# Second mixer: one modulation's weighted sum moved from VectorE to ScalarE and adding transfers

## The reference, cut to what matters

```
c_act = silu(c)                       # 1024 numbers
mod   = c_act @ w_ada + b_ada         # 6 x 1024: shift, scale, gate twice
```

## Time and profile before

| What | us |
|---|---|
| Median of 3 runs | 1464.32 |
| Lowest and highest run | 1462.7, 1465.55 |
| Span of the profiled execution, first to last instruction | 1458.9 |
| PE busy in it | 1373.3 (94%) |
| DVE busy in it | 873.2 (60%) |
| ACT busy in it | 252.0 (17%) |
| POOL busy in it | 258.8 (18%) |

### The profile page before, as it was taken

How to read it: one execution, slowest core, us unless ns; L and a number is a source line. 1 busy time by engine, 2 the same in 40 slices (tenths; PEclk the granted TensorE clock), 3 DMA queues, 4 the chain that set the end, 5 groups by cost and what they waited for, 6 DMA issues and landing times. The chain is left out here.

```text
span 1458.9 us, 18939 instructions
## 1 busy us (share of the span) xinstructions
PE 1373.3 (94%) x7533; PEld 1013.0 (69%) x7533; DVE 873.2 (60%) x1502; ACT 252.0 (17%) x540; POOL 258.8 (18%) x342
## 2 busy tenths in 40 slices
PE   5999999887766999999999999999999999999997
PEld 1877655554433788868888888777776878888843
DVE  2458685442222668763454685788763874777864
ACT  2221121000001211222345101000002113211101
POOL 5078010000000200453355402100020100000000
PEclk9999999998998999999999999999999999999999
DMA  9976878999999598856774455898864552555531
GB/s 350 319 258 229 283 307 347 363 416 415 417 418 378 181 316 277 298 162 164 161 179 132 158 163 175 326 336 311 303 230 141 155 157 80 163 164 171 172 129 46
DMA packets 176055, 355.57 MB, mean 244 GB/s; under 512 B 7289, under 2 KB 137040, under 8 KB 158560
## 3 DMA queue, kind: packets, MB, share of 16 engines
q1 hardware_dynamic: 166720, 313.64, 60.6%
q0 software_dynamic: 9248, 40.71, 9.5%
HBM read 352.58 MB, written 1.74 MB: 243 GB/s over the span
## 5 line engine op out<-in xcount | busy, mean ns | idle before, releaser
L1824 PE MATMUL PS<-HT,ring 128*128 128x256 f32 x1152 | 258.3, 382 | 0.1
L1824 PEld LDWEIGHTS PS<-HT,ring 128*128 128x128 f32 x1152 | 215.4, 190 | 36.0 <-issue 7.9
L1542 DVE TENSOR_TENSOR X<-X,PS 128x1024 f32<-128x1024 f32 x14 | 17.1, 1221 | 112.0 <-PE PS L1318 112.0
L1265 PE MATMUL PS<-ring_extra,slot_rows 128*32 128x256 f32 x576 | 55.2, 440 | 27.7 <-DMA ring_extra<-in_expert_w_gate 7.0
L2758 PE MATMUL PS<-HT,ring 128*128 128x256 f32 x352 | 76.8, 379 | 0.0
L2787 PE MATMUL PS<-ada_stage,half_sums 128*128 128x256 f32 x320 | 75.6, 379 | 0.0
L2787 PE MATMUL PS<-ring,half_sums 128*128 128x256 f32 x320 | 75.6, 379 | 0.0
L2758 PEld LDWEIGHTS PS<-HT,ring 128*128 128x128 f32 x352 | 66.7, 190 | 9.0
L2764 PE MATMUL PS<-ring,hid 128*128 128x512 f32 x160 | 71.8, 592 | 0.0
L2787 PE MATMUL PS<-ring,HT 128*128 128x256 f32 x304 | 68.8, 379 | 0.0
L2787 PEld LDWEIGHTS PS<-ring,half_sums 128*128 128x128 f32 x320 | 59.4, 190 | 11.2 <-issue 4.3
(11 more groups left out here) (713 smaller groups left out, 2450.5 us busy)
## 6 DMA issues: line engine op xcount, KB each, us to landing
ring<-in_hy_w_in SPq DMA_DIRECT2D x40, 1024.0 KB, 7.5
ring_extra<-in_w_ada SPq DMA_DIRECT2D x24, 1024.0 KB, 8.0
ada_stage<-in_ada_w POOLq DMA_DIRECT2D x24, 1024.0 KB, 7.4
ring<-in_ffn_w_gate SPq DMA_DIRECT2D x22, 1024.0 KB, 5.8
ring<-in_ffn_w_up SPq DMA_DIRECT2D x22, 1024.0 KB, 5.7
ring<-in_ffn_w_down SPq DMA_DIRECT2D x22, 1024.0 KB, 6.0
ring_extra<-in_expert_w_down SPq DMA_DIRECT2D x18, 1024.0 KB, 22.9
ring_extra<-in_expert_w_up SPq DMA_DIRECT2D x18, 1024.0 KB, 20.1
```

Of the source, the lines that this page charges most:

```text
L1265: mm = pe.matmul(PS[e * SLOTS:(e + 1) * SLOTS, 2, j * CW:(j + 1) * CW], hs[:, k, e * SLOTS:(e + 1) * SLOTS], w[e][:, k, :], start=(k == 0) ...
L1542: dve.tensor_tensor(part, part, PS[:, 6:8, :], ALU.add).then_inc(added, 1)
L1824: mm = pe.matmul(dst, w[:, k, half * P:(half + 1) * P], HT[:, k, :], start=(k == 0), stop=(k == KT - 1))
```

## The change

The staging place is doubled: `stages` has two, and piece `a` goes to place `a % 2`. Fetch `a` stands one step earlier in SP's list than before. ACT multiplies a piece with its column, in place, at (a + 2, 3), where DVE's `add(a)` was; for k = 0 it writes into `acc` instead. For the 14 pieces with k from 1 to 7, POOL then starts, at the head of the next step, a transfer from the staging place to `acc` that adds at its destination. Fetch `a` waits, for a = 2 and 3, until piece a - 2 has been multiplied into `acc`; from a = 4 on, until the adding transfer of piece a - 2 has landed. PE waits at (19, 2) for the last two adding transfers. DVE's `add` is gone.

```diff
-        stage = sb(scope, "ada_stage", [P, 2 * D])
+        stages = sb(scope, "ada_stage", [P, 2, 2 * D])
+        stage = stages[:, 0]
-        add_at = {(s, 3): s - 2 for s in range(2, 18)}
+        weigh_at = {(s, 3): s - 2 for s in range(2, 18)}
 # SP
-                    for (step_no, _), a in add_at.items():
-                        if step_no == s + (s > 0) or (s == 0 and step_no <= 1):
-                            if a:
-                                sp.wait_ge(summed, a)
-                            sp.dma_start(stage[:].rearrange("p (a n) -> p a n", a=1), wv[:, ds(a // 2, 1), 1 + a % 2, :])\
-                                .then_inc(fetched, 16)
+                    for (step_no, _), a in weigh_at.items():
+                        if step_no == s + (2 if s else 0) or (s == 1 and step_no == 2):
+                            if 2 <= a < 4:
+                                sp.wait_ge(weighed, a - 1)
+                            elif a >= 4:
+                                sp.wait_ge(summed[a % 2], 16 * (a // 2 - 1))
+                            sp.dma_start(stages[:, a % 2:a % 2 + 1, :], wv[:, ds(a // 2, 1), 1 + a % 2, :])\
+                                .then_inc(fetched[a % 2], 16)
 # PE, at (19, 2)
-                        pe.wait_ge(summed, ADDS)
+                        for j in range(2):
+                            pe.wait_ge(summed[j], 16 * (KT - 1))
 # ACT, called at each (s, q) in weigh_at, before that quarter's exponential
+                def weigh(a):
+                    j, k = a % 2, a // 2
+                    act.wait_ge(fetched[j], 16 * (k + 1))
+                    if a == 0:
+                        act.wait_ge(cv_ok, 1)
+                    act.activation(acc[:, j, :] if k == 0 else stages[:, j, :], stages[:, j, :], ACT.Copy,
+                                   scale=cv[:, k:k + 1]).then_inc(weighed, 1)
 # DVE
-                def add(a):
-                    j, k = a % 2, a // 2
-                    dve.wait_ge(fetched, 16 * (a + 1))
...
-                        dve.scalar_tensor_tensor(out=acc[:, j, :], in0=stage[:], scalar=cv[:, k:k + 1], in1=acc[:, j, :],
-                                                 op0=ALU.mult, op1=ALU.add).then_inc(summed, 1)
 # POOL, called at (s, 0) of the step after weigh(a), for a >= 2, ahead of that step's other jobs
+                def add(a):
+                    j, k = a % 2, a // 2
+                    pool.wait_ge(weighed, a + 1)
+                    if k >= 2:
+                        pool.wait_ge(summed[j], 16 * (k - 1))
+                    pool.dma_start(acc[:, j, :], stages[:, j, :], accum_op=ALU.add).then_inc(summed[j], 16)
```

More of the change, by code:

```diff
@@ L1646, in _program @@
         wdt = sb(scope, "w_dt", [P, KT, SSM_H])
-        dt_parts = sb(scope, "dt_parts", [P, S])
+        dt_parts = cum_bias[:, 2016:2016 + S]
         quarter_sum = sb(scope, "quarter_sum", [P, SSM_H])
@@ L1673, in _program @@
         bias_dram = nc.dram_tensor("bias_rows_dram", (ATT_G * KV_H, 384), F32, kind="Internal").ap()
-        small, stored = pool_dma_sem("a_small"), pool_dma_sem("a_stored")
+        small, stored, SMALLS_BEFORE = smalls1, pool_dma_sem("a_stored"), 48
         def small_loads(pool):
@@ L1696, in small_loads @@
                     pool.dma_start(dst, src).then_inc(small, 16)
-        SMALLS = 16 * 16
+        SMALLS = SMALLS_BEFORE + 16 * 16
         xg = carve(x_scores, 0, [TT, D])
@@ L1704, in _program @@
             sem("g_left"), sem("g_right"))
-        late, padded = pool_dma_sem("a_late"), sem("h_padded")
+        padded = sem("h_padded")
         x_squared, x_out = sem("g_xsquared"), sem("o_xout")
@@ L1738, in _program @@
             sem("s_weight"), sem("s_value"), sem("s_ymoved"))
-        cum_out, cum_in = pool_dma_sem("cum_out"), [pool_dma_sem(f"cum_in{j}") for j in range(3)]
-        bias_in = [pool_dma_sem("bias_in0"), pool_dma_sem("bias_in1")]
+        cum_in, CUMS_BEFORE = (smalls2, smalls3, gates_in), (160, 96, 32)
+        bias_in, BIAS_BEFORE = (r_small, pool_dma_sem("bias_in1")), (96, 0)
         scored, biased, maxed, probs, added, scaled, turned, copied, valued, moved_att = (
@@ L1774, in y_block @@
             return YT[:, g * KT + 4 * h:g * KT + 4 * h + 4, i * P:(i + 1) * P]
-        cv_ok, fetched, summed, cols, cols_ok, rows_a, rows_b, gate_ok = (
-            sem("d_c"), sem("d_fetched"), sem("d_summed"), sem("d_cols"),
-            sem("d_colsok"), sem("d_rows_a"), sem("d_rows_b"), sem("d_gates"))
+        cv_ok, fetched, weighed, summed, cols, rows_a, rows_b, gate_ok = (
+            sem("d_c"), [sem("d_fetched0"), sem("d_fetched1")], sem("d_weighed"),
+            [pool_dma_sem("d_summed0"), pool_dma_sem("d_summed1")], sem("d_cols"),
+            sem("d_rows_a"), sem("d_rows_b"), sem("d_gates"))
         row_sums, row_copies = sem("d_rowsum"), sem("d_rowcopy")
@@ L2110, in _ @@
                         act.activation(cv[:], cv[:], ACT.Silu).then_inc(cv_ok, 1)
+                    if (s, q) in weigh_at:
+                        weigh(weigh_at[s, q])
                     if q == 2 and 2 <= s < 2 + NX:
@@ L2246, in setup @@
                     dve.wait_ge(made, 1)
-                    dve.tensor_copy(dt_parts[:], PS[:, 5, 0:S]).then_inc(dt_moved, 1)
+                    dve.tensor_copy(dt_parts, PS[:, 5, 0:S]).then_inc(dt_moved, 1)
                     dve.tensor_copy(convT[:], PS[:, 7, 0:(CONV + 1) * XT])
@@ L2357, in _ @@
                         softplus()
-                    if (s, q) in add_at:
-                        add(add_at[s, q])
                     if (s, q) == (6, 0):
@@ L2374, in _ @@
                         if h < SSM_H:
-                            dve.wait_ge(cum_in[h // 4 % 3], 16 * (h // 12 + 1))
+                            dve.wait_ge(cum_in[h // 4 % 3], CUMS_BEFORE[h // 4 % 3] + 16 * (h // 12 + 1))
                             if h >= 3:
@@ L2387, in _ @@
                         dve.wait_ge(rows_a, 1)
-                        dve.wait_ge(late, 16)
+                        dve.wait_ge(small, SMALLS + 16)
                         dve.tensor_tensor(gate_a[:], gate_a[:], PS[:, 2:4, :].rearrange("p a b -> p (a b)"), ALU.add)\
@@ L2411, in _ @@
                             dve.wait_ge(scored, k + 1)
-                            dve.wait_ge(bias_in[m % 2], 32 * (m // 2 + 1))
+                            dve.wait_ge(bias_in[m % 2], BIAS_BEFORE[m % 2] + 32 * (m // 2 + 1))
                             if k >= 2:
@@ L2478, in load_cums @@
                     if p == 0:
-                        pool.wait_ge(cum_out, 16)
-                        pool.wait_ge(stored, 16)
+                        pool.wait_ge(stored, 32)
                         pool.wait_ge(la_ok, 1)
@@ L2489, in _ @@
                 pool.wait_ge(n_gained, TT)
-                pool.dma_start(gate_a[:], t["ada_b"][0][2 * D:3 * D].partition_broadcast(P)).then_inc(late, 16)
+                pool.wait_ge(small, SMALLS)
+                pool.dma_start(gate_a[:], t["ada_b"][0][2 * D:3 * D].partition_broadcast(P)).then_inc(small, 16)
                 for s, q in QUARTERS:
+                    if (s - 1, 3) in weigh_at and q == 0 and weigh_at[s - 1, 3] >= 2:
+                        add(weigh_at[s - 1, 3])
                     if (s, q) == (2, 0):
@@ L2496, in _ @@
                         pool.wait_ge(cum_mv, 2)
-                        pool.dma_start(cum_dram, cumT[:]).then_inc(cum_out, 16)
+                        pool.dma_start(cum_dram, cumT[:]).then_inc(stored, 16)
                         for p in range(3):
```

## The result

The changed kernel takes 1497.48 us where the kernel before, run beside it, takes 1464.93: a ratio of 1.0232 (95% interval 1.0211 to 1.0254), so it is slower by 2.1 to 2.5%, some 34 us. The ratio is an estimate of its own and not the quotient of the two medians, which is 1.0222, or 32.6 us. The forecast was 1473.9, slower by 9.6. The side was right and the place was right; the forecast was about three and a half times too small.

A forecast was written before the change was run, and what follows sets the result against it. PE was taken to bound the steps the change touches; a 1458.9 us span, 9.6 us of PE waiting on a too-long staging loop and 5.4 up to the runs' median gave 1473.9 us, range 1461.5 to 1511.

The forecast's parts named there:

- PE bounds, DVE's work is worth nothing: Steps from 480 to 640 us: PE sets their time, so taking 36.6 us busy off DVE gains 0.
- ACT's multiplication at 1.9 us: ACT's 16 multiplications of 128x2048: 1.9 us each, bounds 1.3 to 2.4, 30 us on an idle engine, 0 by itself.
- Where PE waits and from what x on: PE waits behind ACT's multiplication of piece 14, latest start 615.8 us; nothing up to x = 15.1, 9.6 us at 16.7.
- x: One turn of the staging loop over two steps, without ACT's 1.9 us multiplication: 16.7 us, from 10.8 to 22.9.
- E: PE's wait from late pieces after six loop turns: 6x - 90.6 us, 9.6 us at x = 16.7.
- The terms of x: Staging loop, issue and landing times in one turn: 0.3 + 9.9 + 0.3 + 6.2 = 16.7 us.
- ACT's end to POOL's issue: Staging loop, from the multiplication's end to the start of the adding transfer: 0.3 us.
- adding transfer, issue to SP's next fetch: Staging loop: 1 MB addition 9.9 us to land, upper bound 14.8; 0.3 for landing to SP's issue and to ACT together.
- fetch, issue to ACT's start: Staging loop, 1 MB fetch beside ring tile and adding transfer: 6.2 us, the middle of 4.9 and 7.5.
- The cross-check by throughput: DMA over 12 steps of 7.9 us: at 418 GB/s 7.5 us a step fits; 10.0 with destination reads costs +18 us.
- what ACT may be late: ACT's multiplication of piece 14 may slip from 608.4 to 615.8 us: 7.4 us taken off the 26 us lack.
- The rival "saturation": DMA transfers in these steps: addition and fetch at upper bounds, x = 22.9, E = 46.8, time 1511 us; chance 0.18.

The follow-up runs named there:

- the third experiment: The changed kernel with ACT multiplying in the two places but DVE adding the product, no adding transfers: 1462.2 us, ratio 0.9989.
- the four places: The changed kernel with four staging places in place of two, a fetch waiting for the adding transfer of piece a - 4: 1493.45 us, ratio 1.0197.
- the kernel with copies: The changed kernel with plain copies in place of the adding transfers, same bytes and waits, no sum: 1473.76 us, ratio 1.0063.

## Why the prediction was off, step by step

**PE bounds, DVE's work is worth nothing: right.** DVE lost 31.2 us of busy time over the whole span (873.2 to 842.0), and nothing became faster; with DVE adding again, the time is that of before.

**ACT's multiplication at 1.9 us: right** (2.00), and harmless, as the third experiment shows.

**Where PE waits and from what x on: right.** The working took the even pieces. The odd ones decide: ACT waited for the landing of each odd piece from 5 to 15. For them the same sum starts at the end of piece 3's multiplication: 521.27 + 1.99 + 5 x 2.0 + 6x. It gives the measured start of piece 15, 658.88, for x = 20.9. Piece 15 stands one step later than piece 14; in the kernel before, PE's heads of that step start at 629.17, and the same count back from there gives about 625 as the latest start. So E is 34 us: that is the loss. By this sum PE waits from x = 15.3 on, where I had 15.1, and my own 16.7 gives 8.5 us. The wait chain, its place, and ACT as the engine behind which it piles up were as forecast.

**The terms of x: the step that failed.** I had 16.7 where 20.9 was measured. The timelines give the starts of the six odd turns: POOL's issues at 523.56, 549.07, 573.62, 594.12, 614.89 and 638.41 us, SP's next fetches at 535.45, 561.95, 584.23, 604.46, 625.06 and 648.89, ACT's multiplications at 546.77, 571.21, 591.83, 612.52, 634.98 and 658.88. The means are:

| Term | Forecast, us | Measured, us |
|---|---|---|
| ACT's end to POOL's issue | 0.3 | 0.5 |
| adding transfer, issue to SP's next fetch | 9.9, and 0.3 for this hop and the next | 11.1 (10.2 to 12.9) |
| fetch, issue to ACT's start | 6.2 | 9.4 (7.6 to 11.3) |

The fetch is the term that failed: 3.2 of the 4.2 us that x was short lie there. I had taken a middle between two landings of a time when no third transfer was there. The addition was 1.2 us longer than 9.9, and between its landing and SP's issue nothing was lost. At six turns, each us of x is 6 us. Behind the sizes stands an idea that failed with them: I took each landing as a length that a transfer has by itself, and the runs showed that in this stage it goes with the sum of engine time that all transfers of a step want.

**The cross-check by throughput: it should have caught this, and failed by its price.** I divided bytes by 418 GB/s, the best rate of any slice, in a stage with other traffic, and got 7.5 to 10.0 us a step. This stage's own rows had the price: two loads took 0.82 of a 7.34 us step, which is 6.0 us of the engines, not the 5.0 that 418 GB/s gives. With a double-priced addition on top a step wants 11. By that I would have written about 30 us and not 18. In both I took 7.4 us off for what ACT may be late; the table above takes nothing off. The decay rows' eight loads, 0.52 MB each, want about 11 us of the same engines and were in no sum of mine; that they use up the allowance is worked out, not shown.

**The rival "saturation" was the mechanism.** It had 0.18 and a price of 46.8, from upper bounds. Its sign was to be ring tiles on which PE waits; they landed late (13.2 us), but with six slots PE never waited for one, and the loss came through ACT. So most of the signs that I had listed for the forecast (ACT's waits for `ada_stage`, PE's gaps ended by ACT and POOL, additions of 10.5 us in the median, a DMA share above 0.95) were there, for another reason than latency: the four places show that. Two were not: the fetch landed after 8.9 us and not about 6, and ACT's waits did not grow from piece to piece (7.41, 14.77, 12.00, 12.02, 9.42 and 9.63 us for the odd ones). That the side and the place came out right under the wrong mechanism was in part luck: both mechanisms delay the landings that ACT waits for.

The Trainium skill's sentence in "DMA: Bandwidth & Descriptors", section "Issuing engines are not separate DMA queues", that transfers of all engines end on the same 16 and interleave, is what these runs show: shares of 55.0 and 48.3% in one window, and a ring tile at 13.2 us. The other sentence that I took from this page of the Trainium skill, section "Anatomy of one DMA", gives by its fit an estimate of 4.4 us for 1 MB. No 1 MB copy or addition here landed so early: the shortest copy took 5.0 us and the shortest addition 7.1, and in the crowded stage the medians were 8.2 and 10.5.

## What to carry to other kernels

Before a transfer is added to a stage, sum the time that the DMA engines are busy there, per step and by the stage's own rows, and add the new one. Where the sum passed the step here (8.4 us and more in steps of 7.9), the landings grew and time was lost, and with four places in place of two at least 25 us of the loss stayed. The weighted sum was taken off an engine that was busy for 115.91 of 160 us and that PE did not wait for, and part of it was put on DMA engines that were busy four fifths of the time: that moved work to the scarcer resource. A transfer that adds at its destination is to be counted for about two copies: 5.1 us of engine time against 2.7 in the crowded stage, 6 against 3.4 in quiet.

## What the runs showed that I had not expected

A wait cost PE more than its length. After its longer waits it ran the next matmuls slower: the granted clock was 1.00 from 563 to 567.6 us, before the wait that ended at 573.84, and 0.50 from 573.8 to 577.5, behind it, which is the lower of the two levels, 1.2 and 2.4 GHz. PE's timeline of the changed kernel has 16 matmuls of one kind before and after a 6.25 us wait:

```profile
563.97 3.62 PE L1828 MATMUL PS<-HT,ring 128*128 128x256 f32 x16
573.84 5.67 PE L1828 MATMUL PS<-HT,ring 128*128 128x256 f32 x16 [6.25 <-ACT rx_zb L2065]
```

Five such places add about 9 us to the 24.7 of waiting, which makes the 34 of the loss as PE's list shows it. As I read it, this is the same loss seen from another side, since the transfers set when the last piece came; no run takes the slower clock out by itself.

POOL's issue of an adding transfer took 0.87 us (median of 14 in the changed kernel), that of a plain copy 0.54 us (median of 14 in the kernel with copies).
